# Scan work shared out anew, two second-mixer stages merged, and constant products on TensorE in waits of the norm and choice stages

## The chip, the cores and the metric

The kernel runs on one core of one Trainium2 chip. The metric is the device time of one execution in microseconds, as the median of several runs. A profile of one execution gives, beside it, what every engine did: TensorE (PE, with its weight loads as PEld), VectorE (DVE), ScalarE (ACT), GpSimd (POOL), SyncE (SP), and the transfers.

## The reference

Two transformer blocks for one sequence of 512 tokens of width 1024, all in float32. The first block's mixer is a neighbourhood attention beside a bidirectional state-space scan; its feed-forward part has 16 experts that each choose 64 tokens. The second block's mixer adds a recurrent branch (RWKV-7, 8 heads of 64) and latent attention (8 heads, causal); its feed-forward part has 4 groups of 8 experts, with one group and two experts a token. The parts that matter here, shortened:

```
# scan, per direction, chunk of 128 tokens and group g (R = 8 heads of 64, state 128)
x = xs * dt;  a = dt * A;  a_cs = cumsum(a)
states = B^T @ (exp(a_cs[-1] - a_cs) * x)              # what a chunk adds to the state
h = exp(a_cs[-1]) * h + states                         # decay, then add
y_diag = (C @ B^T) * exp(segment sums of a, masked) @ x
y_off  = exp(a_cs) * (C @ h_before)
# the context (2 chunks) only sets the first state; the main sequence (4 chunks) gives y

# second mixer
y = groupnorm(rwkv(...)) * gn_w + gn_b + bonus * v;  y = y * g
q_d, kv_d, kr = h @ w_in[:, mla columns]               # "down", 384 + 256 + 32 columns
q = rmsnorm(q_d) @ w_q_up;  kv = rmsnorm(kv_d) @ w_kv_up;  rotary part by cos and sin of positions
u = gate_rw * (y @ w_branch_rw) + gate_mla * (attention(q, kv) @ w_branch_mla);  x = x + u @ w_out

# choices
aff = softmax(h @ w_router); each expert takes its 64 largest of 512 tokens       # first block
group = argmax(softmax(h @ w_group)); the two largest of the group's 8 experts    # second block
```

## The kernel before

The program is a row of stages. A stage (`stage(k, name)`, an `nc.Block`) has one instruction list for each engine, its own tiles in SBUF and PSUM and its own semaphores; at its end the semaphores are freed and all engines meet at a barrier. Inside a stage the lists are written by hand, and only semaphores order them; `Steps` chains each instruction of an engine to the one before. Tiles are laid out with 128 tokens (P) to a partition block; LT = 4 blocks make the sequence, KD = 8 blocks the width. A product of f32 operands shows in the profile as two pairs of weight load and matmul.

**Scan** (`ssd_scan`, from L1226). `units` lists 48 units: for both directions, first two context chunks and then four main chunks, each with 4 groups. `mains` are the 32 main units, `chain` = 8 is the number of units between two of one direction and group (4 groups in 2 directions), so the first 8 units only copy their state product and the other 40 decay and add. For each unit GpSimd writes `seg_in` (main units, L1277: a triangular constant times `a`, 128x1024), `xd` (L1283) and `xde` (L1286). TensorE computes, for main units, `seg` (L1300, 4 matmul records) and `cb` (L1302) one unit ahead, then `st` (L1313, the state product), `yo` (L1318) and the 8 heads' `yd` (L1323). ScalarE exponentiates `seg` into `lx` (L1334). VectorE masks `cb` (L1345), multiplies `lx` by it (L1349), copies (L1354) or decays (L1358) and adds (L1359) the state, and makes y from `off` and `yd` (L1362 to L1371); the second direction has one more add, onto the first direction's y. There are two buffers each of `seg_in`, `xd`, `xde`, `lx`, `off` and one `st`.

**Norm rows** (`RowNorm`, used by the stages `route`, `mixer_rows` and `hm_choose`). VectorE and ScalarE normalize 4 row blocks, the last instruction of each is L322; in the first two stages a branch is added first. `row_ready` counts them. TensorE's `turn` then waits for all four, transposes the 8 column blocks (L370, 4 transposes each) and calls a callback for each, in the choosing stages the scores (L2149, L3318).

**Choices.** `route_tokens`: after the scores VectorE and ScalarE make `aff`, TensorE turns it (L2157), VectorE finds 64 of 512 by rounds of 8 (L2196, L2197), TensorE turns the choice back (L2161) and counts (L2167). `route_experts` (`hm_choose`): VectorE's choices, then TensorE's counts (L3328, L3331). `fine_experts` (`hm`): TensorE makes two lists (L3479), GpSimd gathers rows by indirect transfers (L3462), TensorE turns them (`flips`, L3487) and multiplies with a ring of weights (L3501). The weights of both groups of experts are asked for by SP as early as their buffers allow.

**Second mixer** (`second_mixer`, L3174). Around the change the stages follow in this order: `rw_states` (L2693), `rw_finish` (L2757: VectorE's group norm in 24 us, one square root on ScalarE, the bonus on GpSimd; SP loads the norm rows, the first branch weights into `ahead` and the residual), `rw_y_t` (transposes of y, L402), `rw_br` (branch product, 8 products of 8 records by L526, and multiply onto `uT`, L1539), a load of constants, `p_mla` (the down projection, 8 products of 16 records, width 336), `mla_rows` (L2816: ScalarE's squares, sine and roots, VectorE's rotary tables and normalized rows, 3 tables turned), `mla_qn_t` and `mla_kvn_t` (20 transposes, L402), `mla_up` (L2905, which loads its two weights itself), then attention. `ahead` is a pair of weight buffers that a stage fills for the next one.

## Time and profile before

| what | value |
|---|---|
| median of 3 runs | 3734.84 us (3734.08 to 3745.22) |
| the profiled execution, own time | 3730.5 us |
| its span | 3728.7 us |
| TensorE busy | 3155.3 us, 85% |
| TensorE weight loads | 1675.7 us, 45% |
| VectorE busy | 1146.8 us, 31% |
| ScalarE busy | 478.1 us, 13% |
| GpSimd busy | 320.3 us, 9% |
| instructions | 38059 |
| read from and written to HBM | 653.28 MB, 14.69 MB |

The span runs from the first to the last instruction of the profiled execution; the busy shares are means over stages with different limits. The granted clock of TensorE is given in parts of its full rate: 1.00 is 2.4 GHz and 0.50 is 1.2 GHz. Idle time in brackets stands before an instruction, with what ended it.

### The profile page before, as it was taken

To read this page: it belongs to the slowest core of one execution; us is meant where nothing else is said; L and a number is where in the kernel's file an instruction comes from. 1 tells how busy PE (TensorE), PEld (TensorE's weight loads), DVE (VectorE), ACT (ScalarE), POOL (GpSimd) and SP (SyncE) were. 2 spreads that over 40 slices of the span, in tenths; PEclk is the share of its full clock that TensorE was granted. 3 is DMA by queue.
4 is the path that set the end of the run, shared out by engine and by line. 5 is a ranking of instruction groups with operands and counts; after the bars stand their busy time and mean duration, and the time that the engine had idled before them with its cause. 6 is when DMAs were issued, how large, how long until landed. Compare 5 with 4: busy or idle time off the path is not lost. (4 is left out here: it accounts for less than half of the span.)

```text
span 3728.7 us, 38059 instructions
## 1 busy us (share of the span) xinstructions
PE 3155.3 (85%) x15800; PEld 1675.7 (45%) x15800; DVE 1146.8 (31%) x2119; ACT 478.1 (13%) x898; POOL 320.3 (9%) x261
## 2 busy tenths in 40 slices
PE   6997799996989999598999999987967577995974
PEld 4444545562654444444434443434447443534331
DVE  2234602554893200401011101113264613512112
ACT  1002500111112100100000000001123101301111
POOL 0003000003972000000000000000012100000000
PEclk9998998996999999699999999998989788995997
DMA  6621021100001221399999999995100120015996
GB/s 255 248 68 46 1 71 46 46 23 1 23 1 68 90 68 45 159 410 418 423 416 423 415 428 424 423 388 179 34 1 3 52 76 24 23 45 215 398 425 277
DMA packets 130497, 669.34 MB, mean 180 GB/s; under 512 B 15994, under 2 KB 44061, under 8 KB 97305
## 3 DMA queue, kind: packets, MB, share of 16 engines
q1 hardware_dynamic: 115385, 630.24, 42.1%
q10 hardware_dynamic: 11488, 28.31, 2.0%
q0 software_dynamic: 3456, 8.39, 0.6%
q8 instruction: 125, 2.05, 0.2%
q14 instruction: 43, 0.35, 0.0%
HBM read 653.28 MB, written 14.69 MB: 179 GB/s over the span
## 5 line engine op out<-in xcount | busy, mean ns | idle before, releaser
L1907 PE MATMUL ec_wide<-ec_ring,ec_xg 128*64 128x512 f32 x2048 | 457.9, 601 | 24.3 <-issue 18.6
L1907 PEld LDWEIGHTS ec_wide<-ec_ring,ec_xg 128*64 128x64 f32 x2048 | 148.2, 138 | 313.9 <-issue 309.7
L1941 PE MATMUL ec_acc<-ec_ring,ec_hidT 128*64 128x512 f32 x1024 | 232.8, 608 | 38.4 <-DMA ec_ring<-in_w_exp_down 36.3
L2066 DVE TENSOR_SCALAR ec_xg<-ec_piece,ordered 128x128 f32<-128x128 f32 x64 | 21.9, 404 | 583.0 <-PE ec_piece L1955 583.0
L1941 PEld LDWEIGHTS ec_acc<-ec_ring,ec_hidT 128*64 128x64 f32 x1024 | 84.5, 140 | 184.6 <-issue 184.6
L3501 PE MATMUL hm_gu<-hm_ring,hm_xg 128*64 128x512 f32 x480 | 110.8, 615 | 23.7 <-DMA hm_ring<-in_moe_w_gu 22.3
L1955 PE MATMUL ec_piece<-ec_sel,x 128*128 128x128 f32 x512 | 124.4, 405 | 3.3 <-DVE ec_sel L2048 3.3
L1955 PEld LDWEIGHTS ec_piece<-ec_sel,x 128*128 128x128 f32 x512 | 122.9, 336 | 9.1 <-issue 5.7
L2631 POOL TENSOR_TENSOR solve_T<-const_rw,solve_T 128x512 f32<-128x512 f32 x8 | 10.1, 1266 | 1330.2 <-DVE solve_T L2669 1330.2
L1107 PE MATMUL conv_main<-hT,conv_early 128*128 128x512 f32 x192 | 85.3, 599 | 1.6 <-DVE bcT L1183 1.6
L526 PE MATMUL p_rkv_acc<-ahead_rkv,h2mT 128*128 128x384 f32 x256 | 84.5, 494 | 2.3 <-DVEq L534 2.3
L1107 PE MATMUL conv_main<-hT,conv_late 128*128 128x512 f32 x192 | 85.8, 600 | 0.0
L2030 ACT ACTIVATE ec_hidT<-ec_acc 128x512 f32<-128x512 f32 x32 | 17.4, 594 | 519.3 <-PE ec_acc L1930 519.3
L3501 PEld LDWEIGHTS hm_gu<-hm_ring,hm_xg 128*64 128x64 f32 x480 | 39.2, 141 | 94.3 <-issue 92.5
L1277 POOL TENSOR_TENSOR ssd_seg_in<-const_all,a 128x1024 f32<-128x1024 f32 x32 | 77.3, 2416 | 0.6 <-PE ssd_cb L1302 0.6
L2081 DVE TENSOR_TENSOR branch<-branch,ec_piece 128x512 f32<-128x512 f32 x64 | 44.0, 687 | 107.2 <-PE ec_piece L1973 107.2
L1973 PE MATMUL ec_piece<-ec_y,ec_selT 128*128 128x512 f32 x128 | 63.8, 622 | 7.3 <-DVE ec_selT L2075 6.1
L1286 POOL TENSOR_TENSOR ssd_xde<-ssd_xd,dec 128x512 f32<-128x512 f32 x48 | 68.7, 1431 | 3.8
L1300 PE MATMUL ssd_seg<-ssd_seg_in,const_all 128*128 128x512 f32 x128 | 62.4, 610 | 4.7 <-DVE ssd_cbm L1345 4.7
L526 PEld LDWEIGHTS p_rkv_acc<-ahead_rkv,h2mT 128*128 128x128 f32 x256 | 49.4, 193 | 37.0 <-DVEq L534 2.5
L2676 DVE TENSOR_TENSOR solve_T<-solve_T,solve_wide 64x512 f32<-64x512 f32 (+1 forms) x80 | 50.5, 632 | 50.0 <-PE solve_wide L2562 42.0
L1358 DVE TENSOR_TENSOR ssd_state<-ssd_state,dec 128x512 f32<-128x512 f32 x40 | 59.7, 1492 | 18.4 <-PE ssd_st L1313 18.4
(620 smaller groups left out, 5016.5 us busy)
## 6 DMA issues: line engine op xcount, KB each, us to landing
ec_ring<-in_w_exp_gate SPq DMA_DIRECT2D x64, 2048.0 KB, 14.0
ec_ring<-in_w_exp_up SPq DMA_DIRECT2D x64, 2048.0 KB, 22.2
ec_ring<-in_w_exp_down SPq DMA_DIRECT2D x64, 2048.0 KB, 17.7
hm_ring<-in_moe_w_gu SPq DMA_DIRECT2D x30, 2048.0 KB, 18.8
hm_ring<-in_moe_w_down SPq DMA_DIRECT2D x15, 2048.0 KB, 15.9
ahead_qkv<-in_w_in SPq DMA_DIRECT2D x10, 2048.0 KB, 9.6
key<-in_w_ada ACTq DMA_DIRECT2D x4, 2048.0 KB
v<-in_w_ada ACTq DMA_DIRECT2D x4, 2048.0 KB, 10.2
```

What stands on the lines that cost most here:

```text
L526: last = pe.matmul(acc[0:rows, bank, 0:cols], stat(j), mov(j), start=(j == 0), stop=(j == kt - 1))
L1107: last = pe.matmul(main[:, i % 2, :], w[:, j, m * P:(m + 1) * P], hT[:, j, :], start=(j == 0), stop=(j == KD - 1))
L1277: pool.tensor_tensor(seg_in[:, m % 2], cum.unsqueeze(1).to_broadcast([P, HG, P]), spread(a[:, tile(u), hs:hs + HG], P), ALU.mult).then_inc ...
L1286: pool.tensor_tensor(xde[:, n % 2].rearrange("p (h e) -> p h e", h=HG), xd[:, n % 2].rearrange("p (h e) -> p h e", h=HG), spread(e2, 64), ...
L1300: pe.matmul(seg[:, h, :], k.const("after" if d == 0 else "before"), seg_in[:, m % 2, 4 * h:4 * h + 4].rearrange("p h l -> p (h l)"), start ...
L1358: link(dve.tensor_tensor(sv, sv, spread(e3, 64), ALU.mult))
L1907: last = pe.matmul(wide[half(e), b, :], xg[:, u % 2, j, half(e)], w[e][:, a, b * 512:(b + 1) * 512], start=(j == 0), stop=(j == KD - 1))
L1941: last = pe.matmul(acc[half(e), h, :], hidT[:, f, half(e)], w[e][:, r, h * 512:(h + 1) * 512], start=(f == 0), stop=(f == FT - 1))
L1955: last = pe.matmul(piece[:, m % 2, i * P:(i + 1) * P], x[:, t, HALF * h + i::KD], sel[:, t, :], start=(t == 0), stop=(t == LT - 1))
L1973: pe.matmul(piece[:, m % 2, :], selT[:, t * P:(t + 1) * P], y[:, h * 512:(h + 1) * 512], start=True, stop=True).then_inc(piece_done, 1)
L2676: dve.tensor_tensor(x, x, wide[s][half(c), c, first * 256:512], ALU.subtract).then_inc(T_done[s], 1)
L3501: last = pe.matmul(gu[half(e), u % 2, :], xg[:, u % 2, j, half(e)], w[e][:, j, :], start=(j == 0), stop=(j == KD - 1))
```

## The change

Three parts. **Scan:** `seg_in` is written by ScalarE, two units ahead, as eight 128x128 activations with a per-partition scale; the state decay goes from VectorE to GpSimd, between the inputs of the next unit and those after it, with a semaphore of its own; the last 8 units, whose state nobody reads, have no `xde`, no state product and no state update. **Second mixer:** SP issues the down weights, the norm rows, positions, constants and residual during `rw_states`; one stage, `rw_finish_and_down`, has the down projection on TensorE, ScalarE's copies of it and the norm on VectorE; a second, `rw_branch_and_rows`, has y's transposes, the branch products, the tables, the normalized rows and all turns, with the branch weights, the two `mla_up` weights and the gate weights asked for by its SP. Seven stages and a load become two stages; two barriers are new in `latent_attention` and `second_mixer`. **Constant products:** `keep_warm(n)` issues n products of `ones` and `ident`, whose result nobody reads, while TensorE waits: after the first, second and third ready row (20 each in `route` and `mixer_rows`, 6 each in `hm_choose`), 12 before `aff`, 72 before the choice, 48 before the counts of `hm_choose` and 64 before the flips of `hm`.

```diff
+def keep_warm(k, pe, bank, n):
+
+    for _ in range(n):
+        pe.matmul(bank[:, 0:P], k.const("ones"), k.const("ident"), start=True, stop=True)
...
+        for t in range(LT - 1):
+            pe.wait_ge(self.row_ready, t + 1)
+            keep_warm(self.k, pe, self.pt[:, 3, :], 20 if self.branch is not None else 6)
...
-            m = 0
-            for n, u in enumerate(units):
-                main, d, c, g = u
+
+            def inputs(n):
+                main, d, c, g = units[n]
                 x = (xs if main else xsc)[:, c, g * GW:(g + 1) * GW].rearrange("p (h e) -> p h e", h=HG)
                 hs = d * SSD_H + g * HG
-                if main:
-                    if m >= 2:
-                        pool.wait_ge(seg_ready, m - 1)
-                    cum = k.const("upto" if d == 0 else "from")
-                    pool.tensor_tensor(seg_in[:, m % 2], cum.unsqueeze(1).to_broadcast([P, HG, P]),
-                                       spread(a[:, tile(u), hs:hs + HG], P), ALU.mult).then_inc(seg_built, 1)
                 if n >= 2:
-                    pool.wait_ge(state_ready, n - 1)
+                    if n - 2 < kept:
+                        pool.wait_ge(state_ready, n - 1)
                     if n - 2 in mains:
                         pool.wait_ge(diag_ready, mains.index(n - 2) + 1)
-                link(pool.tensor_tensor(xd[:, n % 2].rearrange("p (h e) -> p h e", h=HG), x,
-                                        spread(dt[:, tile(u), hs:hs + HG], 64), ALU.mult))
-                e2 = dec[:, d * N_SEG + tile(u), 32 + g * HG:32 + (g + 1) * HG]
+                ins = pool.tensor_tensor(xd[:, n % 2].rearrange("p (h e) -> p h e", h=HG), x,
+                                         spread(dt[:, tile(units[n]), hs:hs + HG], 64), ALU.mult)
+                if n >= kept:
+                    ins.then_inc(inputs_ready, 1)
+                    return
+                link(ins)
+                e2 = dec[:, d * N_SEG + tile(units[n]), 32 + g * HG:32 + (g + 1) * HG]
                 pool.tensor_tensor(xde[:, n % 2].rearrange("p (h e) -> p h e", h=HG),
                                    xd[:, n % 2].rearrange("p (h e) -> p h e", h=HG), spread(e2, 64),
                                    ALU.mult).then_inc(inputs_ready, 1)
-                m += main
+
+            def decayed(n):
+                main, d, c, g = units[n]
+                if main:
+                    pool.wait_ge(off_ready, mains.index(n) + 1)
+                pool.wait_ge(state_done, n - chain + 1)
+                e3 = dec[:, d * N_SEG + tile(units[n]), 64 + g * HG:64 + (g + 1) * HG]
+                sv = state[:, d, g, :].rearrange("p (h e) -> p h e", h=HG)
+                pool.tensor_tensor(sv, sv, spread(e3, 64), ALU.mult).then_inc(state_decayed, 1)
+
+            inputs(0)
+            for n in range(len(units)):
+                if n + 1 < len(units):
+                    inputs(n + 1)
+                if chain <= n < kept:
+                    decayed(n)
...
+                if n < kept:
+                    if n >= 1:
+                        pe.wait_ge(state_done, n)
+                    pe.matmul(st[:, :], (b_rows if main else bc_rows)[:, c, g * P:(g + 1) * P], xde[:, n % 2, :], start=True,
+                              stop=True).then_inc(state_ready, 1)
+                else:
+                    pe.wait_ge(state_done, n - chain + 1)
...
+            def segment_inputs(m):
+                main, d, c, g = units[mains[m]]
+                if m >= 2:
+                    act.wait_ge(seg_ready, m - 1)
+                cum = k.const("upto" if d == 0 else "from")
+                for h in range(HG):
+                    col = d * SSD_H + g * HG + h
+                    ins = act.activation(seg_in[:, m % 2, h, :], cum, ACT.Copy, scale=a[:, tile(units[mains[m]]), col:col + 1])
+                ins.then_inc(seg_built, 1)
+
+            segment_inputs(0)
+            segment_inputs(1)
             for m in range(len(mains)):
                 act.wait_ge(seg_ready, m + 1)
                 if m >= 2:
                     act.wait_ge(diag_ready, m - 1)
                 act.activation(lx[:, m % 2].rearrange("p (b h) l -> p b (h l)", b=2), seg[:, :, :], ACT.Exp).then_inc(exped, 1)
+                if m + 2 < len(mains):
+                    segment_inputs(m + 2)
...
-                dve.wait_ge(state_ready, n + 1)
+                if n < kept:
+                    dve.wait_ge(state_ready, n + 1)
                 if n < chain:
                     dve.tensor_copy(state[:, d, g, :], st[:, :]).then_inc(state_done, 1)
-                else:
-                    e3 = dec[:, t, 64 + g * HG:64 + (g + 1) * HG]
-                    sv = state[:, d, g, :].rearrange("p (h e) -> p h e", h=HG)
-                    link(dve.tensor_tensor(sv, sv, spread(e3, 64), ALU.mult))
+                elif n < kept:
+                    dve.wait_ge(state_decayed, n - chain + 1)
                     dve.tensor_tensor(state[:, d, g, :], state[:, d, g, :], st[:, :], ALU.add).then_inc(state_done, 1)
...
+            keep_warm(k, pe, norm.pt[:, 0, :], 12)
             pe.wait_ge(aff_ready, 1)
...
+            keep_warm(k, pe, norm.pt[:, 0, :], 72)
             pe.wait_ge(chosen_T, 1)
...
+        @block.tensor
+        def _(pe):
+            for i, (c, t) in enumerate(tiles):
+                if t == 0:
+                    pe.wait_ge(down_loaded[c], 16)
+                if i >= 4:
+                    pe.wait_ge(product_taken, i - 3)
+                for j in range(KD):
+                    last = pe.matmul(acc[:, i % 4, 0:width], hT[:, j, t * P:(t + 1) * P], down_w[:, c, j * width:(j + 1) * width], start=(j == 0), stop=(j == KD - 1))
+                last.then_inc(product_ready, 1)
+
         @block.scalar
         def _(act):
-            act.wait_ge(var_ready, 1)
-            act.activation(var[:, :, :], var[:, :, :], ACT.Sqrt, scale=1.0 / 64, bias=k.const("gn_eps")).then_inc(root_ready, 1)
+            for i, (c, t) in enumerate(tiles):
+                act.wait_ge(product_ready, i + 1)
+                act.activation(down[:, t, c * width:(c + 1) * width], acc[:, i % 4, 0:width], ACT.Copy).then_inc(product_taken, 1)
+                if i == 2:
+                    act.wait_ge(var_ready, 1)
+                    act.activation(var[:, :, :], var[:, :, :], ACT.Sqrt, scale=1.0 / 64, bias=k.const("gn_eps")).then_inc(root_ready, 1)
+            act.wait_ge(product_taken, len(tiles))
...
+            for b in range(2):
+                ahead.load_first(sp, b, k.dram["w_branch_rw_2"][0], NY, 512)
+            for (dst, src), up_loaded in up_moves:
+                sp.dma_start(dst, src).then_inc(up_loaded, 16)
+            for b in range(2):
+                sp.wait_ge(product_ready, 4 * (b + 1))
+                ahead.load_first(sp, b, *w_next)
...
+            merge(0)
...
+            for j in range(NY):
+                turn(j, lambda t: y[:, t, j * P:(j + 1) * P], P).then_inc(y_flipped, 1)
+            pe.wait_ge(y_taken, NY)
+            for m in range(3):
+                product(m)
             pe.wait_ge(table_ready, 2)
             for i in range(3):
-                for t in range(LT):
-                    last = pe.transpose(bank[0:MLA_QK, i, t * P:(t + 1) * P], table[:, i, t, :], k.const("ident"))
-            last.then_inc(flipped, 1)
-
-
-def mla_up(k, qnT, kvnT, cT, sT, krT, qT, kT, v):
+                turn(i, lambda t: table[:, i, t, :], MLA_QK).then_inc(flipped, 1)
+            product(3)
+            for i, (dst, scale, j) in enumerate(columns):
+                source = qn if i < MLA_Q // P else kvn
+                pe.wait_ge(normed, LT if i < MLA_Q // P else 2 * LT)
+                if i:
+                    pe.wait_ge(flip_taken, i)
+                turn(3 + i, lambda t: source[:, t, j * P:(j + 1) * P], P).then_inc(flipped, 1)
+                if i in (1, 3):
+                    product(4 + i // 2)
+            product(6)
+            product(7)
...
+                    def late_loads(sp):
+                        for b in range(2):
+                            source = w_down.rearrange("(k p) n -> p k n", p=P)[:, :, b * (n_down // 2):(b + 1) * (n_down // 2)]
+                            sp.dma_start(down_w[:, b].rearrange("p (k n) -> p k n", k=KD), source).then_inc(down_loaded[b], 16)
+                        for dst, name in zip(norm_rows, ("rw_gn_w_2", "rw_gn_b_2")):
+                            sp.dma_start(dst[:, :], k.dram[name][0:1, :].to_broadcast([P, RW_D])).then_inc(norm_loaded, 16)
+                        sp.dma_start(pos_i[:, :], k.dram["positions_2"].rearrange("a (t p) -> p (a t)", p=P),
+                                     allow_slow_non_contiguous=True).then_inc(positions_loaded, 16)
+                        sp.dma_start(*mla_const).then_inc(mla_const_loaded, 16)
+                        sp.dma_start(k.residual.tile[:, :, :], rows_view(x_in)).then_inc(k.residual.loaded, 16)
+                        sp.wait_ge(mla_const_loaded, 16)
+
+                    rw_states(k, MT, N, D_next, GT, K_[:, :, :].rearrange("p t (c q n) -> p (t c) q n", q=RW_PAIRS, n=64), y, late_loads)
+                    rw_finish_and_down(k, y, z, g, bonus, Q, norm_loaded, norm_rows, hT, (down_w, down_loaded), down)
...
-                rw_finish(k, y, z, g, bonus, branch_loads)
...
-                yT = tile(s, "rw_yT", [P, RW_D // P, L])
-                transpose_rows(k, "rw_y_t", y, LT, RW_D // P, yT)
-                branch(k, "rw_br", k.dram["w_branch_rw_2"][0], RW_D // P, yT, uT, None, False, ahead, (w_down, KD, n_down // 2))
...
+            keep_warm(k, pe, norm.pt[:, 0, :], 48)
             pe.wait_ge(chosen_ready, 1)
...
+            pe.wait_ge(index_ready, 2)
+            keep_warm(k, pe, list_, 64)
             flips(0)
```

## Rows read from the trace of the kernel before

**Rows 1.** The page, section 2: busy tenths of the transfers in 40 slices.
```profile
DMA  6621021100001221399999999995100120015996
```

**Rows 2.** Stretch, us, busy (count) of PE, PEld, DVE, ACT, POOL; clock, DMA share, GB/s.
```profile
939.00:1036.00 97.00, 96.69 (x453) 61.72 (x453) 85.57 (x106) 18.42 (x18) 89.65 (x53) 1.00 0.00 1
...
1515.40:1535.80 20.40, 20.27 (x96) 19.77 (x96) 3.26 (x5) 4.39 (x5) 0.00 (x0) 0.50 0.86 367
...
2549.00:2553.80 4.80, 4.76 (x23) 4.76 (x24) 1.69 (x3) 1.37 (x2) 0.00 (x0) 0.50 0.00 0
2553.80:2555.90 2.10, 1.35 (x11) 1.11 (x10) 1.31 (x2) 1.37 (x2) 0.00 (x0) 0.95 0.00 0
```

**Rows 3.** Timeline, context units of the scan: start, duration (us), operation, idle before.
```profile
902.31 0.69 DVE L1354 COPY ssd_state<-ssd_st 128x512 f32<-128x512 f32 x1 [2.30 <-PE ssd_st L1313]
905.30 1.56 DVE L1358 TENSOR_TENSOR ssd_state<-ssd_state,dec 128x512 f32<-128x512 f32 x1 [2.30 <-PE ssd_st L1313]
...
909.88 1.56 DVE L1358 TENSOR_TENSOR ssd_state<-ssd_state,dec 128x512 f32<-128x512 f32 x1 [2.30 <-PE ssd_st L1313]
...
905.27 1.04 POOL L1283 TENSOR_TENSOR ssd_xd<-xsc,dt 128x512 f32<-128x512 f32 x1 [0.82 <-PE ssd_st L1313]
```

**Rows 4.** Timelines, main units of the scan, by engine.
```profile
944.07 1.02 ACT L1334 ACTIVATE ssd_lx<-ssd_seg 128x1024 f32<-128x1024 f32 x1 [2.63 <-PE ssd_cb L1302]
...
1031.17 1.02 ACT L1334 ACTIVATE ssd_lx<-ssd_seg 128x1024 f32<-128x1024 f32 x1 [4.42 <-PE ssd_cb L1302]
1037.16 1.02 ACT L1334 ACTIVATE ssd_lx<-ssd_seg 128x1024 f32<-128x1024 f32 x1 [4.97 <-PE ssd_cb L1302]
...
1126.71 1.02 ACT L1334 ACTIVATE ssd_lx<-ssd_seg 128x1024 f32<-128x1024 f32 x1 [6.09 <-PE ssd_cb L1302]
...
1071.95 0.68 DVE L1358 TENSOR_TENSOR ssd_state<-ssd_state,dec 128x512 f32<-128x512 f32 x1
...
1077.72 2.38 DVE L1358 TENSOR_TENSOR ssd_state<-ssd_state,dec 128x512 f32<-128x512 f32 x1
...
1076.68 2.88 POOL L1277 TENSOR_TENSOR ssd_seg_in<-const_all,a 128x1024 f32<-128x1024 f32 x1
...
1003.64 1.87 PEld L1323 LDWEIGHTS ssd_yd<-ssd_xd,ssd_lx 128*128 128x128 f32 x16
```

**Rows 5.** Timeline, from the states to latent attention, and the weights' landing.
```profile
2959.05 2.29 DVE L2797 TENSOR_REDUCE rw_fin_mean<-rw_y 128x32 f32<-128x2048 f32 x1 [1.65 <-PEq L3247]
...
2970.48 0.32 ACT L2792 ACTIVATE rw_fin_var<-rw_fin_var,const_all 128x32 f32<-128x32 f32 x1 [10.19 <-DVE rw_fin_var L2802]
...
2984.30 3.49 PE L402 MATMUL rw_y_t_pt<-const_all,rw_y 128*128 128x128 f32 x16 [27.69 <-PEq L209]
...
2989.54 2.81 PE L526 MATMUL rw_br_b_acc<-rw_yT,ahead 128*128 128x512 f32 x6 [1.75 <-DVEq L534]
...
3025.34 3.14 PE L526 MATMUL p_mla_acc<-ahead,h2mT 128*128 128x336 f32 x5 [8.10 <-DVEq L534]
...
3063.31 0.51 DVE L546 COPY mla_down<-p_mla_acc 128x336 f32<-128x336 f32 x1 [4.01 <-PE p_mla_acc L526]
...
3100.02 4.55 PE L2946 MATMUL mla_up_pq<-mla_qnT,mla_up_wq 128*96 128x512 f32 x6 [10.94 <-DMA mla_up_wkv<-in_mla_w_kv_up]
...
ahead<-in_w_in SPq DMA_DIRECT2D x2, 1344.0 KB, 5.8
```

**Rows 6.** Timeline: the first ready row, and waits of TensorE in the choosing stages.
```profile
1505.89 0.75 DVE L322 TENSOR_SCALAR branch<-x,ec_rstd 128x1024 f32<-128x1024 f32 x1
...
1537.40 1.02 PE L2157 MATMUL route_wide<-const_all,ec_aff 128*16 128x128 f32 x4 [1.59 <-DVE ec_aff L2190]
...
1551.84 0.60 PE L2161 MATMUL route_score<-const_all,route_chosenT 16*128 16x16 f32 x4 [13.42 <-DVE route_chosenT L2198]
...
3392.76 1.49 PE L3328 MATMUL hm_choose_count<-hm_choose_chosen,const_all 128*128 128x32 f32 x6 [9.03 <-DVE hm_choose_chosen L3389]
...
3419.97 1.97 PE L3487 MATMUL hm_flip<-const_all,hm_xrow 128*128 128x128 f32 x8 [10.06 <-DMA hm_xrow<-hm_xn_rows,hm_index]
```

155 lines of the change are left out of this document (93 added, 62 removed).

## The prediction

> **What bounds the kernel now.** I read the page first: no engine is busier than TensorE (the table above), but the transfers fill slices 18 to 25 and 37 to 38 whole [rows 1]. Those are the two groups of expert stages, in which the weights' transfer is the bound. A stage in front of them that ends later or earlier moves them whole, because their buffers are full by then and the queue stands; no delay ahead of them is made good behind them. Next I cut the run at the stages that the change touches [rows 2]. In the scan's first half TensorE is busy 96.7 of 97 us; in the route stage's turn and scores it is busy throughout at a granted clock of 0.50 (1.2 GHz). The second mixer's turn starts at 0.50 and reads 0.95 after 2553.8. Then I read the timelines: the scan's context units [rows 3] and main units [rows 4], the way from the second mixer's states to latent attention's first product [rows 5], and the waits of TensorE that the constant products are to fill [rows 6].
>
> **Rates.** A 128x128 f32 product is two records (the steps of one f32 product); so one record each counts below. At the raised clock 16 records take 1.87 us [rows 4], 0.117 each; at 0.50 96 take 20.27 [rows 2], 0.211 on the mean and 0.22 by the gap-free ones among them. So a constant product costs 0.23 us raised and 0.44 low.
>
> **A, the scan.** (1) *Context units.* For the first eight, which only copy, starts lie 2.99 apart; for the eight that decay, 4.58 (905.30 to 909.88), with the decay at 1.56 in the chain of VectorE and TensorE [rows 3]. With the decay on GpSimd the chain is the copy's 2.99 again, since the add costs as the copy, but GpSimd must do three multiplies of one size, for which I take the 1.04 of the one in these rows [rows 3], and 0.2 between them: 3.3. The bound above is the decay at VectorE's 1.56, and the other way the copy's 2.99. So 8 x (4.58 - 3.3) = -10; bounds -6 and -13. (2) *Main units, first half.* 16 periods from 944.07 to 1031.17 are 5.44 each [rows 4], and TensorE has no gap [rows 2]: nothing is gained. GpSimd loses 2.3 us of segment inputs and gains 1.04 of decay; what hides it is TensorE's own 5.44. (3) *Second half.* 13 periods from 1037.16 to 1126.71 are 6.89 each [rows 4]. There VectorE has one more add, and its two-input operations stretch: the decay takes 0.68 at 1071.95, and 2.38 at 1077.72 while GpSimd's 1024-wide multiply runs from 1076.68 for 2.88 [rows 4]. Removed are that multiply and the decay. In the first half VectorE keeps TensorE's pace of 5.44 with all of these operations but one, and the decay goes, so 5.44 would be the bound here too; but the mask, for which TensorE waits, stands behind the additional add, and for that I put 0.5 (the add is no longer than the 0.68 of the decay alone): 5.95. 16 x 0.93 = -15; bounds 0 and -23. The last eight units' missing state products give nothing in this sum: VectorE's order sets them. (4) *ScalarE.* It takes eight 128x128 activations a unit. None of this size and form stands in these rows: the 128x32 one takes 0.32 [rows 5] and the 128x1024 one 1.02 [rows 4]. I take 0.35, near the small one by size: 8 x 0.35 + 1.02 = 3.8, inside the 5.44 of TensorE, and two units ahead. At the other end, 1.02, it is 9.2 (see the rivals). A together: **-25**, bounds -15 and -33 (the ends aren't met together).
>
> The Trainium skill ("SBUF — State Buffer", the two sides) says that VectorE's two-input operations and GpSimd's reads take one port pair as an exclusive lock, for a whole instruction. The 2.38 beside the 0.68 agrees. It speaks against the move as well: decay on GpSimd locks VectorE out for its whole length.
>
> **B, the second mixer.** Before, the way is a chain without overlap: VectorE's finish starts at 2959.05 and hands on at 2984.30; y's transposes; branch products from 2989.54, which end at 3025.34 - 8.10 = 3017.24; a load and 8.10 idle; the down projection from 3025.34 to 3063.31; the rows and tables, two transposing stages, and a wait of 10.94 for weights that only mla_up asks for, to 3100.02 [rows 5]. From 2957.4 (the last product of the states) that is 142.6. After: the finish's stage starts at 2958.4 (one barrier less before it). TensorE's 64 products of 336 columns take 38.0 (3063.31 - 3025.34), to 2996.3, ScalarE's last copy to 2996.9. VectorE's 24.4 lies beside it; its root, at 2970.48 before [rows 5], now waits for ScalarE's third copy at 2958.4 + 3 x 4.74 + 0.5 = 2973 or later, 2.5 to 4.3 late: VectorE ends by 2987.7, hidden by 9 us. Two barriers: 2998.5. Now SP issues the branch weights, which stood loaded before: 1344 KB takes 5.8 to land [rows 5]; I take 5.5 for the 1024 KB, so 3004.0 (below: 3.5, what 16 transposes at 0.22 need anyway; above: 7.5). Eight products took 27.7 (2989.54 to 3017.24); 12 + 20 transposes at 0.112 to 0.23 add 3.6 to 7, waits and the low clock's start 1 to 2: 3037. The tables' chain (ScalarE's squares, table load and sine, VectorE's rows) starts when the stage does. In these rows it stands with two transposing stages and their barriers between 3063.8 and 3100.02 - 10.94 = 3089.1 [rows 5], 25.3 in all, which bounds it; I take 14 of them, to 3012.5. The third product ends at 3004.0 + 3 x 3.46 = 3014.4, so it is hidden, but by little. Last merge and barrier: mla_up starts at 3038.7, its weights asked for long before. So -61.3; two more barriers inside latent attention +1.8, and mla_up's first products at the raised clock -1.6: **-61**, bounds -50 (tables 11 late at 25.3) and -64 (weights at 3.5).
>
> **C, the constant products.** *Cost.* In route and mixer TensorE is free for products when the first row is ready: 1505.89 + 0.75 = 1506.64 [rows 6]; the turn starts at 1515.4 [rows 2]. Sixty products, the first 8 to 15 low, take 15.1 to 16.8, longer than the 8.8 of the rows: the turn is 6.3 to 8 late, I take 7.2, in each of the two stages (the mixer's has the same spacing). The choice's 18 products: 2.4 late (1.6 to 3.3). The 12 behind the scores (2.7 raised) stand against a wait of 1.59 [rows 6]: +1.8 with a slower hand-over (1.1 to 3.7). The 72 take 16.5 against 13.42: +3.5 (2.7 to 6). The 48 take 10.8 against 9.03: +1.8. The 64 behind the lists take 16 to 17.7 against 10.06: +7.0 (6 to 8) [rows 6]; VectorE's gathered rows are late by as much. Together 30.9. *Return.* If the clock is up when the turn starts, the 20.3 us of turn and scores shrink [rows 2]; 12 records a tile at 0.117 and two hand-overs make about 11.6, but a dip is likely: -6 in route and -8 in the choice stage (-2 to -8.7 each). The mixer's turn, 6.1 to 6.8, falls to 4.3: -2.5, as the 0.95 after 2553.8 shows a raised turn to go [rows 2]. The counts behind 72 and 48: -2.2, -2.7. The flips, and the experts' first products behind 64: -3.4; p_rkv's first: -0.9. Together -25.7. Net **+5**, bounds -8 and +20.
>
> The Trainium skill ("TensorE: Matmul & The Clock Gate", LDWEIGHTS) states that loading the stationary operand takes its columns over 1.2 in ns, without the clock in it. By it a turn, half loads, would give back little. Here 16 load records took 1.87 us at clock 1.00 and 96 took 19.77 at 0.50, 0.117 and 0.206 each [rows 2, 4], so the trace disagrees; by the rule the sum would be some 18 higher.
>
> **Sum.** -25 - 61 + 5 = -81. The profiled execution took 3730.5 by its own clock (span 3728.7): 3649.5. The runs' median, 3734.84, lies 4.3 above it: **3652**.
>
> **Rivals.** (1) *The clock gives nothing back* (this is the change not doing what it says): 30.9 is paid and the 25.7 lost, +26: 3678. For it: the score stage stayed at 0.50 with TensorE busy throughout [rows 2]. Against it: the mixer's transposes raised it to 0.95 [rows 2]. 0.12. (2) *The scan yields only its context part*: GpSimd's decay, multiply and multiply (3.1 at least) meet VectorE's two-input operations in the second half and stretch them as the 2.38 does [rows 4]; the period stays 6.7: 16 x 0.75 lost, 3664. 0.12. (3) *The merged stage waits*, for its tables or the branch weights: B is -45, 3668. 0.08. (4) *Better*: A at -33 and C at -4: 3635. 0.05. (5) *Slower*: ScalarE bounds the scan. At 1.02 an activation [rows 4] a unit takes 9.3; 32 units make 298 for the 197 of now, +101 on -56 - 10: 3770. It decides from 0.92 each, where 8 x 0.92 + 1.02 + 0.2 = 8.6 a unit eats the other gains and 11 us. Against it: 0.32 for the small one [rows 5]. 0.03, and 0.01 for a size between.
>
> **How the numbers follow.** The forecast has 0.59; its own range is 3638 to 3668. For 8 in 10 the range takes in rivals 2 to 4 and most of 1: 3626 to 3686 (A, B and C at their low ends are -105, 3630, less 4 if the median lies no higher than the profiled execution; B at -50 and C at +20 with A at -19 are 3686). 0.3% is 11 us, about what a measurement of this kernel can tell from no change. Only rival 5 reaches that: faster 0.96, same 0.01, slower 0.03.
>
> **What would show it.** A: context units at 3.3, main units at 5.44 and 5.95, ScalarE's activations at 0.35; wrong if ScalarE has no idle time or the second half reads 6.7. B: the down projection beside the finish, 38 us; third branch product before the tables; mla_up's first product 81 us after the states' last; wrong if TensorE idles before the tables' turn. C: granted clock near 1.00 in turn and scores and the route's turn late by 7; wrong if the clock there reads 0.50, or if the idle of TensorE before the counts stays. The prediction fails most easily at C's return and at the second half of the scan.

## The result, and the profile after

The changed kernel takes 3647.07 us (median of 4, 3644.0 to 3661.75) where the kernel before takes 3736.16 on the same chip: ratio 0.9765, 95% interval 0.9733 to 0.9796, so faster by 2.0 to 2.7%. The forecast was 3652, range 3626 to 3686. Executions of one kernel differ by up to 19 us; so single parts of the change are read from the stages of the traces, and the medians only for what is larger.

The page after, its first section, and the granted clock by slices:

```profile
span 3642.8 us, 39461 instructions
PE 3197.3 (88%) x16452; PEld 1725.6 (47%) x16452; DVE 1071.7 (29%) x2059; ACT 559.0 (15%) x1166; POOL 274.7 (8%) x253
PEclk9998998997999999999999999998998989998997
```

TensorE has 652 matmul records more and 42 us more busy time in a span 86 us shorter. The constant products are 668 records and 85.1 us of it (16 records of state products are gone, and the other records took 43 us less); busy time is no gain in itself. ScalarE went from 478.1 to 559.0, GpSimd from 320.3 to 274.7, VectorE from 1146.8 to 1071.7.

Where the span's 85.9 us come from, by the same marks in both traces (a fourth row is the end of the norm's last instruction; the other marks are starts; the first experts end with their last `ec_acc` product, the second with the output's last row; the states' last product and `mla_up` are TensorE's):

| stretch | before | after | difference | forecast |
|---|---|---|---|---|
| scan, start to first `lx` (context part) | 63.37 | 53.22 | -10.15 | -10 |
| to the 18th `lx` (first half) | 90.75 | 91.01 | +0.26 | 0 |
| to the 32nd `lx` (second half) | 95.54 | 83.60 | -11.94 | -15 |
| to the last head products | 6.45 | 7.54 | +1.09 | 0 |
| route, fourth row to the first gather | 45.14 | 43.45 | -1.69 | +4.3 |
| first experts | 956.41 | 952.34 | -4.07 | 0 |
| mixer, fourth row to `p_rkv` | 8.46 | 13.92 | +5.46 | +3.8 |
| states' last product to `mla_up` | 143.6 | 82.3 | -61.3 | -61.3 |
| `mla_up` to attention's turned output | 159.76 | 163.25 | +3.49 | +0.2 |
| choice, fourth row to the lists | 42.49 | 33.85 | -8.64 | -6.5 |
| lists to the first expert product | 17.40 | 23.73 | +6.33 | +3.6 |
| second experts | 299.81 | 295.44 | -4.37 | 0 |

The last column has the terms of the prediction put to these marks; what the table leaves out, -0.3, is spread over the stages between.

The context units after, GpSimd's timeline, beside [rows 3]:

```profile
903.51 1.04 POOL L1306 TENSOR_TENSOR ssd_state<-ssd_state,dec 128x512 f32<-128x512 f32 x1
904.51 1.04 POOL L1288 TENSOR_TENSOR ssd_xd<-xsc,dt 128x512 f32<-128x512 f32 x1
905.63 1.04 POOL L1295 TENSOR_TENSOR ssd_xde<-ssd_xd,dec 128x512 f32<-128x512 f32 x1
906.63 1.04 POOL L1306 TENSOR_TENSOR ssd_state<-ssd_state,dec 128x512 f32<-128x512 f32 x1
```

GpSimd has no gap; three multiplies make a unit, 3.12 us instead of 4.58. The second half after, beside [rows 4], TensorE, VectorE, GpSimd and ScalarE:

```profile
1054.18 1.96 PE L1324 MATMUL ssd_seg<-ssd_seg_in,const_all 128*128 128x512 f32 x4 [0.31 <-DVE ssd_cbm L1386]
...
1101.77 1.96 PE L1324 MATMUL ssd_seg<-ssd_seg_in,const_all 128*128 128x512 f32 x4 [1.10 <-DVE ssd_cbm L1386]
...
1052.20 0.69 DVE L1410 TENSOR_TENSOR ssd_off<-ssd_off,ssd_yd 128x512 f32<-128x512 f32 x1
1052.92 0.91 DVE L1411 TENSOR_TENSOR y<-y,ssd_off 128x512 f32<-128x512 f32 x1
1053.75 0.28 DVE L1386 TENSOR_TENSOR ssd_cbm<-ssd_cb,const_all 128x128 f32<-128x128 f32 x1
...
1054.69 2.02 POOL L1306 TENSOR_TENSOR ssd_state<-ssd_state,dec 128x512 f32<-128x512 f32 x1
...
1050.40 1.02 ACT L1373 ACTIVATE ssd_lx<-ssd_seg 128x1024 f32<-128x1024 f32 x1 [2.64 <-PE ssd_cb L1326]
1051.32 2.43 ACT L1364 ACTIVATE ssd_seg_in<-const_all,a 128x128 f32<-128x128 f32 x8
1056.39 1.02 ACT L1373 ACTIVATE ssd_lx<-ssd_seg 128x1024 f32<-128x1024 f32 x1 [2.64 <-PE ssd_cb L1326]
```

A unit is 5.99 here and 5.97 on the mean of the stretch. The last periods, whose units have no state product, are 5.93: TensorE's gap there is 1.10, again up to the mask, so that leaving these products out gave next to nothing here. ScalarE's eight small activations take 2.43 together, 0.30 each, and it is idle for 2.64 a unit. In the units before, TensorE's one gap is 0.31 and ends with the mask, which stands behind two adds of VectorE.

The merged stages, TensorE's timeline, beside [rows 5]:

```profile
2936.97 36.40 PE L2839 MATMUL rw_fin_acc<-rw_T,h2mT 128*128 128x336 f32 x128 [1.84 <-PEq L209]
2975.49 2.86 PE L2988 MATMUL mla_rows_flip<-const_all,rw_y 128*128 128x128 f32 x16 [2.12 <-PEq L3383]
2981.01 13.30 PE L2998 MATMUL mla_rows_acc<-mla_o,ahead 128*128 128x512 f32 x24 [2.66 <-DMA ahead<-in_w_branch_rw]
2994.15 1.47 PE L2988 MATMUL mla_rows_flip<-const_all,mla_v 128*96 128x128 f32 x12
2995.46 3.60 PE L2998 MATMUL mla_rows_acc<-mla_o,ahead 128*128 128x512 f32 x8
...
3017.21 3.62 PE L3058 MATMUL mla_up_pq<-mla_qnT,mla_wq 128*96 128x512 f32 x4 [2.23 <-PEq L209]
```

TensorE is idle for 1.84, 2.12, 2.66 and 2.23 us, at the three boundaries and for the branch weights, 8.9 of the 82.3 us. The tables are turned at 2994.15 without a wait. The turn and the scores of both choosing stages, busy time by stretch beside [rows 2] (first the bursts in front of them):

```profile
1484.80:1499.90 15.10, 15.06 (x121) 15.06 (x122) 7.89 (x12) 3.36 (x9) 0.00 (x0) 0.89 1.01 430
1499.90:1511.10 11.20, 10.66 (x98) 10.33 (x96) 3.25 (x4) 4.01 (x5) 0.00 (x0) 1.00 1.01 430
...
3285.80:3296.90 11.10, 10.69 (x98) 10.38 (x97) 3.00 (x4) 3.65 (x5) 0.00 (x0) 1.00 0.99 392
```

20.3 us have become 11.2 at a granted clock of 1.00. The turn starts 6.3 us after the fourth row in route and 7.7 in the mixer.

### The profile page after: what moved, and what is told of

Same layout as the page of the kernel before. It is cut to its first block and busy times, and to the rows that moved or that the text cites. A ratio compares the mean times of both kernels' runs of the same rounds, so it can differ in the third digit from the quotient of the medians.

```text
span 3642.8 us, 39461 instructions
## 1 busy us (share of the span) xinstructions
PE 3197.3 (88%) x16452; PEld 1725.6 (47%) x16452; DVE 1071.7 (29%) x2059; ACT 559.0 (15%) x1166; POOL 274.7 (8%) x253
## 5 line engine op out<-in xcount | busy, mean ns | idle before, releaser
L1981 PE MATMUL ec_acc<-ec_ring,ec_hidT 128*64 128x512 f32 x1024 | 233.9, 611 | 36.4 <-DMA ec_ring<-in_w_exp_down 34.2
L1364 ACT ACTIVATE ssd_seg_in<-const_all,a 128x128 f32<-128x128 f32 x256 | 77.8, 390 | 1.8 <-PEq L1766 1.8
L1350 PE MATMUL ssd_yd<-ssd_xd,ssd_lx 128*128 128x64 f32 x512 | 62.1, 275 | 2.1 <-DVE ssd_lx L1390 2.1
L535 PE MATMUL na_br_g_acc<-hT,ahead_na 128*128 128x512 f32 x128 | 57.2, 610 | 7.1 <-ACTq L543 7.1
## 6 DMA issues: line engine op xcount, KB each, us to landing
ec_ring<-in_w_exp_down SPq DMA_DIRECT2D x64, 2048.0 KB, 17.5
hm_ring<-in_moe_w_down SPq DMA_DIRECT2D x15, 2048.0 KB, 15.3
v<-in_w_ada ACTq DMA_DIRECT2D x4, 2048.0 KB, 10.2
```

Source lines behind the costliest of these rows:

```text
L535: last = pe.matmul(acc[0:rows, bank, 0:cols], stat(j), mov(j), start=(j == 0), stop=(j == kt - 1))
L1350: last = pe.matmul(yd[:, m % 2, h * 64:(h + 1) * 64], lx[:, m % 2, h, :], xd[:, n % 2, h * 64:(h + 1) * 64], start=True, stop=True)
L1364: ins = act.activation(seg_in[:, m % 2, h, :], cum, ACT.Copy, scale=a[:, tile(units[mains[m]]), col:col + 1])
L1981: last = pe.matmul(acc[half(e), h, :], hidT[:, f, half(e)], w[e][:, r, h * 512:(h + 1) * 512], start=(f == 0), stop=(f == FT - 1))
```

## The experiments

All start from the changed kernel. Marks as in the table above.

**No constant products** (`a1_no_constants`):

```diff
-    for _ in range(n):
+    for _ in range(0):
```

> All constant products out, the rest of the changed kernel kept. Theory 1 (what the stages of the trace after show is all they do: route -1.7, mixer +5.5, choice stage up to the first expert product -2.3, so +1.5 net; the 4.1 and 4.4 us by which the two expert stretches are shorter have another cause): 3646, and both expert stretches stay short. Theory 2 (the shorter expert stretches come from them as well, -8.5 more): 3654, and the first expert stretch is back at 956 us, the second at its old length. The forecast's +5 would make it 3642.

Measured: 3653.0, ratio 0.9767 (0.9745 to 0.9790), the same as with them. Route 45.21 (43.45 with them), mixer 9.08 (13.92), choice 42.68 (33.85), lists to first expert product 17.37 (23.73): in these stages the constant products cost 0.6 us altogether, so they give and take in about equal parts. The experts' stretches are 959.7 and 296.6. The second stayed short, against theory 2. The first is nearly what theory 2 has (956), and so is the median (3654), but this decides nothing: with the products in, other traces of the changed kernels have 951.7 to 965.7 there. Turn and scores are back at 20.3 and 0.50:

```profile
1494.70:1515.00 20.30, 20.25 (x96) 19.73 (x96) 3.24 (x4) 4.39 (x5) 0.00 (x0) 0.50 0.89 376
```

**No 64 before the flips** (`a2_no_64`):

```diff
-            keep_warm(k, pe, list_, 64)
```

> Only the 64 products before the first flips out. Theory 1 (forecast: a delay in front of the experts is carried to the end): flips 7.3 us earlier, flips and first products 3.3 slower at the low clock, end 4 earlier: 3643. Theory 2 (the ring's transfers start with the stage and are the bound from there, so that a late flip is made good): the first expert product is 4 us earlier and the end is where it was, 3647 within 1.

Measured: ratio 0.9767 (0.9747 to 0.9787). Lists to the first expert product 17.31 instead of 23.73, lists to the end of the second experts' stretch 311.8 instead of 319.2: the 6.4 us stay won, so theory 1, with more than the 4 us of its sum. With the 64 products the flips (1.06 for 8 records, 1.94 here) and the first experts' products are faster, but the end is no earlier for it. TensorE waits for the gather again as in [rows 6]:

```profile
3334.27 1.94 PE L3615 MATMUL hm_flip<-const_all,hm_xrow 128*128 128x128 f32 x8 [10.00 <-DMA hm_xrow<-hm_xn_rows,hm_index]
```

The median, 3647.9, doesn't show it; with 4 executions 6 us can't be told from chance.

**No burst in the mixer** (`a3_no_mixer_burst`) and **bursts of 8** (`a4_burst_of_8`):

```diff
-            keep_warm(self.k, pe, self.pt[:, 3, :], 20 if self.branch is not None else 6)
# a3 (only route has a shift)
+            keep_warm(self.k, pe, self.pt[:, 3, :], 20 if self.shift is not None else 0 if self.branch is not None else 6)
# a4
+            keep_warm(self.k, pe, self.pt[:, 3, :], 8 if self.branch is not None else 6)
```

> The 60 products of the second mixer's norm stage out, those of the route stage kept. Theory 1 (they are 7.7 us late and give back 2.4 in the turn and under 1 behind it): the way from the fourth row to the first p_rkv product is 8.5 us instead of 13.9 and the end 4.5 to 5.5 earlier: 3642. Theory 2 (what follows is bound by a load, not by TensorE): no change of the end, 3647.

> Bursts of 8 instead of 20 in the route and mixer stages: 8 products at the low clock are 3.6 us, the spacing of the rows, so the third burst ends 2 us behind the fourth row. Theory 1 (that is enough for the clock): turn and scores stay at 11.3 us in route and 3.7 in the mixer, both turns start 4 to 5.5 us earlier: 3638. Theory 2 (the clock is not up at the turn): turn and scores take 15 to 20 us again, the mixer's turn 5 to 6: 3647 to 3650.

Measured: 3645.9 and 3648.8, ratios 0.9766 (0.9738 to 0.9793) and 0.9758 (0.9736 to 0.9780), neither to be told from the changed kernel. By the traces the mixer's way is 8.41 with none (9.08 in `a1_no_constants`), 6.65 with 8 (in three traces) and 12.4 to 14.2 with 20 (in eight). So 8 are enough there, and the other 12 only delay. In route, in the one trace with 8, the stage took 45.45; the clock fell among the scores, 0.63 on the mean:

```profile
1495.40:1512.40 17.00, 16.53 (x98) 16.30 (x98) 3.24 (x4) 4.39 (x5) 0.00 (x0) 0.63 1.00 424
```

Theory 1 holds for the mixer. For route this trace is as theory 2 has it; but with 20 the clock falls among the scores too in some traces (see `c1_joined`), so one trace doesn't show that 8 are too few.

**Decay back on VectorE** (`s1_decay_on_vector`):

```diff
-                if chain <= n < kept:
-                    decayed(n)
...
-                    dve.wait_ge(state_decayed, n - chain + 1)
+                    link(dve.tensor_tensor(sv, sv, spread(e3, 64), ALU.mult))
```

> The state decay back on VectorE, the segment inputs still on ScalarE. Theory 1 (the forecast's shares: the decay's move made the context part, the segment inputs' move the second half): context part 10 us longer again, first half at 5.44 a unit, second half at 6.0 to 6.7 because the decay costs VectorE 0.7 alone and meets a shorter GpSimd load; end 10 to 21 later: 3657 to 3668. Theory 2 (it is the pair that counts: without the 1024-wide multiply GpSimd hardly stands in VectorE's way and the second half needs nothing else): second half stays at 5.97, 3657.

Measured: ratio 0.9796 (0.9780 to 0.9813), 3657.9. Context part 63.33, as before the change; first half 90.75; second half 83.51, as after it. That is theory 2. VectorE's decay, with GpSimd's 1024-wide multiply gone:

```profile
1049.68 1.75 DVE L1388 TENSOR_TENSOR ssd_lx<-ssd_lx,ssd_cbm 128x1024 f32<-128x1024 f32 x1
1051.35 0.68 DVE L1398 TENSOR_TENSOR ssd_state<-ssd_state,dec 128x512 f32<-128x512 f32 x1
...
1048.98 1.37 POOL L1295 TENSOR_TENSOR ssd_xde<-ssd_xd,dec 128x512 f32<-128x512 f32 x1
```

It takes 0.68 in each of the second half's seven decays, where it alternated between 0.68 and 2.38 in [rows 4]. In the context part and the first half it still takes 1.56 and 1.48 on the mean, as before, beside GpSimd's other multiplies. So the segment inputs' move made the second half without the decay's. The reverse case is the next run.

**Segment inputs back on GpSimd** (`s2_segments_on_gpsimd`), decay there too:

```diff
+                    if n + 1 in mains:
+                        seg_inputs(mains.index(n + 1))      # the 128x1024 multiply of before
...
-                    segment_inputs(m + 2)
```

> The segment inputs back on GpSimd as one 1024-wide multiply, the decay still on GpSimd. Theory 1 (GpSimd becomes the bound: 2.3 + 1.0 + 1.4 + 1.4 a unit and blocking): context part as after, first half 6.2 to 6.6 a unit instead of 5.46, second half 6.9 to 7.5: 3676 to 3690. Theory 2 (TensorE and VectorE still bound the first half, since the inputs are made ahead): first half 5.5, second half as before the change, 6.9: 3659.

Measured: ratio 0.9817 (0.9794 to 0.9840), 3671.5. Context 53.53, first half 96.93, second half 89.98. The periods are 5.84 in the first half, 6.29 in the second as long as units have a state product, and 6.56 in the last ones. Neither theory has these numbers: the second half is shorter than theory 2's 6.9 and theory 1's range. Up to the last units GpSimd is busy without a gap (139.2 of 141.4 us), which is theory 1's cause at less than its price:

```profile
1054.21 1.89 POOL L1305 TENSOR_TENSOR ssd_seg_in<-const_all,a 128x1024 f32<-128x1024 f32 x1
1056.06 1.04 POOL L1288 TENSOR_TENSOR ssd_xd<-xs,dt 128x512 f32<-128x512 f32 x1
1057.18 1.37 POOL L1295 TENSOR_TENSOR ssd_xde<-ssd_xd,dec 128x512 f32<-128x512 f32 x1
1058.51 2.02 POOL L1315 TENSOR_TENSOR ssd_state<-ssd_state,dec 128x512 f32<-128x512 f32 x1
```

In the last units GpSimd is idle half the time (22.1 of 45.0 us busy); there VectorE's multiply, beside the 1024-wide one of GpSimd, and the mask hold the unit:

```profile
1095.31 2.34 POOL L1305 TENSOR_TENSOR ssd_seg_in<-const_all,a 128x1024 f32<-128x1024 f32 x1
...
1096.13 2.60 DVE L1397 TENSOR_TENSOR ssd_lx<-ssd_lx,ssd_cbm 128x1024 f32<-128x1024 f32 x1
```

So the decay's move without the segment inputs' gives the context part (-9.8) and, with the last units' missing state work, 5.6 us of the second half, but costs 6.2 in the first: it needs the segment inputs' move, and not the other way round.

**The mask's wait later** (`s3_mask_wait_later`):

```diff
                     pe.wait_ge(exped, m)
-                    pe.wait_ge(masked, m)
...
+                if m >= 1:
+                    pe.wait_ge(masked, m)
                 pe.matmul(cb[:, 0:P], bT...
```

> TensorE's wait for the mask moved from in front of the two segment products to in front of the product of C and B, the only one that needs it. Theory 1 (what holds the second half at 5.97 is the chain last head product, two VectorE adds, mask, segment products): the period falls to between 5.5 and 5.75, the second half is 4 to 7 us shorter: 3641 to 3644. Theory 2 (VectorE's multiply of the masked tile, 1.75 to 2.0 behind the mask, comes last anyway): 5.9 to 5.97, no gain.

Measured: 3645.8, ratio 0.9748 (0.9731 to 0.9766); the median doesn't show it, and the trace lost 4.5 us again in its route stage (47.93). Second half 76.47 instead of 83.60, the last unit 0.85 longer: -6.3. The mean period is 5.46, but no unit has it: the units with a state product take 5.77 and the last ones, without, 5.18. In the former TensorE has no gap (38.6 of 39.0 us busy) and is the bound again; in the latter it waits 0.33 for VectorE's multiply. So the chain of theory 1 did hold the second half, and 5.3 of the 7.1 us came in the last seven periods, where leaving out the state product, which had given nothing, now counts.

```profile
1083.78 2.00 PE L1351 MATMUL ssd_yd<-ssd_xd,ssd_lx 128*128 128x64 f32 x16 [0.33 <-DVE ssd_lx L1391]
```

**Tables first** (`b1_tables_first`):

```diff
-            for m in range(3):
-                product(m)
             pe.wait_ge(table_ready, 2)
             for i in range(3):
                 turn(i, ...)
-            product(3)
+            for m in range(4):
+                product(m)
```

> In the merged stage the three tables are turned before the first branch product and not behind the third. Theory 1 (the tables' chain of ScalarE and VectorE is ready 7.8 us after the weights, and only the three products hide it): the first branch product starts at about 2990.3 instead of 2981.0, mla_up 7.8 us later: 3655. Theory 2 (the chain isn't on the path, TensorE has room later in the stage): mla_up at most 2 later, 3648.

Measured: ratio 0.9791 (0.9771 to 0.9811), 3660.9. States to `mla_up` 91.27 instead of 82.30, +9.0. Theory 1. The median is 14 above that of the changed kernel; what is beyond the 9 lies in stages with the same code (the first experts took 965.7 in this trace). The two waits of TensorE, and its start on `mla_up`:

```profile
2995.24 2.92 PE L2988 MATMUL mla_rows_flip<-const_all,rw_y 128*128 128x128 f32 x16 [2.12 <-PEq L3382]
3008.73 2.77 PE L2988 MATMUL mla_rows_flip<-const_all,mla_v 128*96 128x128 f32 x12 [10.57 <-DVE mla_v L2961]
...
3044.24 1.93 PE L3057 MATMUL mla_up_pq<-mla_qnT,mla_wq 128*96 128x512 f32 x4 [2.23 <-PEq L209]
```

The 10.57 us now stand in the open, and after them the turns run at the low clock (2.77 for what took 1.47).

**One barrier less** (`b2_one_barrier`):

```diff
-        nc.clear_and_free_semaphores([up_loaded])
-        nc.all_engine_barrier(sem_only=True)
...
-                nc.clear_and_free_semaphores([norm_loaded, ...
+                nc.clear_and_free_semaphores([up_loaded, norm_loaded, ...
```

> The barrier between mla_up and attention out, its semaphore freed with the others behind attention. Theory 1 (the added barrier makes TensorE's idle time there longer, the clock falls, and attention's first scores and gate products take twice their time): from mla_up's first product to the transposes of attention's output 160.3 to 161 us instead of 163.25, back near the 159.8 of before. Theory 2 (a barrier costs its own time alone): 162.3 to 162.9.

Measured: 3644.5, ratio 0.9749 (0.9724 to 0.9773); the stretch is 160.31 instead of 163.25. Theory 1. The start of attention, first after the change, then here:

```profile
3071.87 1.59 PE L3125 MATMUL mla_score<-mla_kT,mla_qT 96*128 96x128 f32 x4 [2.15 <-PEq L3239]
...
3075.57 3.46 PE L1635 MATMUL mla_gate_acc<-h2mT,ahead 128*128 128x512 f32 x4
```

```profile
3079.26 0.89 PE L3125 MATMUL mla_score<-mla_kT,mla_qT 96*128 96x128 f32 x4 [1.78 <-PEq L209]
...
3081.95 1.88 PE L1635 MATMUL mla_gate_acc<-h2mT,ahead 128*128 128x512 f32 x4
```

With an idle time of 2.15 instead of 1.78 us everything behind it takes nearly twice its time for about 7 us: a barrier of 0.4 us cost 2.9. This isn't chance: all ten traces with the barrier have the 2.15 and a clock of 0.50 behind it, and the three without it, and the kernel before, have 1.78 to 1.80 and no fall.

**Down projection after the finish** (`b3_down_after_finish`):

```diff
+            pe.wait_ge(finished, 1)          # VectorE, behind its last operation
             for i, (c, t) in enumerate(tiles):
...
+            act.wait_ge(var_ready, 1)        # the root, ahead of the copies and no longer behind the third
+            act.activation(var[:, :, :], var[:, :, :], ACT.Sqrt, ...
```

> In the first merged stage TensorE waits with the down projection until VectorE has finished the norm (the root goes ahead of ScalarE's copies). Theory 1 (the overlap with VectorE's 24.4 us is that much of the gain): states' last product to mla_up's first 82.3 + 24.4 = 107, end 3671. Theory 2 (most of the gain is from boundaries and waits, the overlap brings less since two engines in one stage slow each other): under 100.

Measured: ratio 0.9826 (0.9806 to 0.9845), 3671.5. States to `mla_up` 109.41, +27.1: theory 1, a little more than VectorE's 24.4. Of the -61.3 that is 27. The rest stands in [rows 5] as `mla_up`'s wait (10.9), the idle 8.1, the rows and turns that now lie between the products, and boundaries; no run takes these apart.

**Joined** (`c1_joined`: mask later, no 64, bursts of 20 in route and 8 in the mixer, one barrier less; `c2_joined_14`: 14 in route):

> The changed kernel with the mask's wait later (-6.3 in the stages of its own trace), no 64 products before the flips (-6.4), bursts of 8 in the mixer's norm (-6.6) and one barrier less (-2.4 by theory 1 of that run, -0.6 by theory 2). If the stages add, about 21 us below the changed kernel: 3626, ratio 0.970. Rival (the gains are lost in the expert stretches, whose transfers vary by more): ratio 0.975.

> The same with bursts of 14 instead of 20 in the route stage: 42 products end 3.8 us earlier. Theory 1 (14 keep the clock up through turn and scores as 20 do): from the fourth row to the first gather product 39.6 instead of 43.45. Theory 2 (the clock falls among the scores, as with 8): 42 to 45.5.

Measured: 3633.4 and 3634.1, ratios 0.9725 (0.9708 to 0.9743) and 0.9734 (0.9712 to 0.9755), the lowest of all; the first lies between the full sum (0.970) and its rival (0.975). By their own stages the scan, the mixer (6.65), the barrier (160.30) and the flips (17.5) gave what they had given alone. Of the 21 us 14 came by the medians and 9 by the profiled spans, since in this trace route took 48.01 instead of 43.45 and the first experts 959.8 instead of 952.3. With 14 route took 48.70: the clock fell among the scores, as in theory 2, but the stage is 3 us beyond the range of that theory. The route stage of `c1_joined`:

```profile
1496.90:1509.00 12.10, 11.56 (x99) 11.23 (x98) 3.24 (x4) 4.39 (x5) 0.00 (x0) 0.93 0.83 351
1509.00:1514.00 5.00, 5.00 (x24) 5.00 (x25) 1.07 (x5) 0.26 (x1) 3.51 (x1) 0.50 0.00 0
```

The clock fell inside the scores. It is not the other edits: among the ten traces with 20 in route, six have bursts of 15.2 to 15.3 us together and then a stage of 43.45 to 43.50, and four have 15.4 to 16.6 and a stage of 47.05 to 48.01; the four include runs that change the scan or the second mixer alone. Busy time by stretch around the rise and the fall, first the changed kernel, then `c1_joined`:

```profile
1484.90:1488.10 3.20, 3.20 (x15) 3.20 (x16) 3.10 (x4) 1.01 (x3) 0.00 (x0) 0.50 1.03 440
1488.20:1535.80 47.60, 44.60 (x398) 43.88 (x397) 22.86 (x49) 7.56 (x13) 3.51 (x1) 1.00 0.50 210
```

```profile
1480.50:1486.60 6.10, 6.08 (x28) 6.08 (x29) 5.89 (x8) 1.90 (x6) 0.00 (x0) 0.50 1.01 432
1486.80:1507.10 20.30, 19.83 (x181) 19.59 (x179) 5.07 (x8) 4.40 (x7) 0.00 (x0) 1.00 0.98 416
1507.30:1513.90 6.60, 6.60 (x31) 6.60 (x32) 1.07 (x5) 1.50 (x2) 3.51 (x1) 0.50 0.02 7
```

In the six the clock rose 3.3 to 3.4 us after the first constant product and stayed up through turn, scores and choice. In the four it rose after 3.7 (`b1_tables_first`) or 6.1 to 6.2 us and fell 9.0 or 10.2 us into turn and scores. Why one execution goes the one way and the next the other isn't shown.

## Why the prediction was right, and where it was off

**What held.** The merged mixer is right in its sum (-61.3) and in its mechanisms: VectorE done 8 us ahead of TensorE, its root 4.2 late behind the third copy, the first branch product 5.2 us after the issue of its weights, tables hidden (`b1_tables_first`: +9.0 when they aren't, 7.8 expected), the overlap worth the finish (`b3_down_after_finish`). That the sum is right to a tenth is luck: the down projection took 36.4 for the 38.0 of the forecast, and from the first branch product to `mla_up` it was 36.2 for 34.7. The context units (3.3 expected, 3.12), the second half's period (5.95, 5.97), ScalarE's small activations (0.35, 0.30) and the turn's lateness (7.2; 6.3 and 7.7) are close. Rivals 2, 3 and 5 are refuted: the second half did not stay at 6.7, the merged stage did not wait for its tables and waited for the branch weights no longer than was priced, and ScalarE idles for 2.6 us a unit. That a delay in front of the second experts is carried whole is shown by `a2_no_64`; for the first experts, whose stretch differs by 14 us between traces, no run shows it.

**What was mis-sized.** (1) Scan: -25 was taken, -20.75 came. The difference of periods was right (0.93 taken, 0.92 measured), but I multiplied it by 16 where only the 13 periods from 1037.16 on were long before [rows 4], which gives the -11.9, and the last unit became 1.1 longer. (2) "Two more barriers inside latent attention +1.8, and mla_up's first products at the raised clock -1.6": the second did not come (the first 6 records took 4.48 us, 4.55 before), the first was 3.5, since behind one of the barriers the clock fell. (3) The return in turn and scores was taken at 6 and 8 of at most 8.7 because "a dip is likely"; it was 9.1 and 9.3 in this trace, and what stands behind the scores in route cost 2 us less than was taken. Against that, the mixer's burst of 20 cost 1.7 more, and the 64 products 2.7 more: of the 3.4 that they were to give back, 0.9 came in the flips, and the experts' faster products brought the end no nearer. So C came out at +1.5 by the table (+0.6 beside `a1_no_constants`) and not +5. Over the ten traces with 20 in route that stage takes 45.2 on the mean (six at 43.5, four near 47.7), which is what it takes without any (45.2). So the dip exists, in 4 of 10 executions, and a forecast that allowed for it was not wrong to; no length of burst is seen to pay in route on the mean.

Against the forecast these three are +4, +3 and -4. What makes the measured time shorter than the forecast all the same are the experts' stretches, 4.1 and 4.4 us shorter than before, for which nothing was forecast. That is luck: without it the median would read about 3655, still inside the range. The first of the two stretches reads between 951.7 and 965.7 in the traces of changed kernels, with the same code; so the 956.4 of before is inside that spread and nothing is to be credited. The second reads 293.4 to 296.6 in all of the changed kernels' traces and 299.8 in the one trace of before. `a1_no_constants` shows that most of it is not the constant products (296.6); what it is stays open, and one trace of before can't tell it from chance. The 3652 itself doesn't follow from the sum either: -81 on the median of 3734.84 is 3653.8, and nothing in the working takes the other 1.8 off. One reading of [rows 1] is wrong and changes nothing: the transfers fill slices 18 to 27 and 38 to 39, not 18 to 25 and 37 to 38.

**The clock.** The first rival (clock gives nothing back, 0.12) is refuted by the 11.2 us at 1.00, and by `a1_no_constants`: what the products cost came back but for 0.6. The weight loads shrank with the clock: 96 records took 19.77 us at 0.50 [rows 2] and 10.33 at 1.00, 0.206 and 0.108 each. The Trainium skill's rule for them ("TensorE: Matmul & The Clock Gate", LDWEIGHTS), which has no clock in it, gives for 128 columns an estimate of 107 ns; that agrees at 1.00 and not at 0.50, so the measurement decides. With the 1024-wide multiply off GpSimd, VectorE's decay took 0.68 throughout the second half (`s1_decay_on_vector`), and 1.48 to 1.56 where GpSimd's other multiplies stand beside it. The Trainium skill's rule on the shared port ("SBUF — State Buffer", the two sides) agrees with that.

## What to carry to other kernels

Cut a trace at marks that both kernels have before believing a total: here one part of the change (the constant products) was worth nothing beside two that were worth 21 and 58, and two of its places (the mixer's bursts of 20 and the 64) cost more than they gave. Products that only keep a clock up must fit in the wait that they fill: three bursts of 8 in the mixer's 8.8 us gave 1.8 to 2.4 us, of 20 cost 3 to 6; 64 in a wait of 10 cost 6.4. Fitting isn't enough, though: in route 8 ended 0.4 us behind the fourth row and gave nothing in the one trace. When two engines exchange work, ask of each move alone which stretch it serves; and look at which single instruction a wait really guards, since moving one wait by two lines gave 6.3 us, most of it by making good on work that had been left out before without any gain.

## What the runs showed of the hardware

The rise of the clock is not tied to the program: with the same instructions in route it came 3.3 to 3.4 us after the first constant product in six executions, which kept it through turn and scores, and after 3.7 to 6.2 us in four, in which it fell to 0.50 again 9.0 to 10.2 us into them. In front of attention an idle time of 2.15 us was followed by work at half speed in ten traces of ten, and one of 1.78 to 1.80 in none of four. The length alone doesn't decide: behind the same 2.23 us in front of `mla_up` its first 4 records took 3.62 in the changed kernel and 1.93 in `b1_tables_first`. Eight 128x128 activations with a per-partition scale take 0.30 each when they follow one another, close to the 0.32 of one of 128x32 [rows 5]. GpSimd's 128x1024 multiply took between 1.89 and 2.88 us both before and in `s2_segments_on_gpsimd` (2.31 and 1.89 on the mean of the first half), and its 128x512 decay 1.04 in the context units and up to 2.02 in the main ones, where VectorE has more work: one operation of one shape has no one price.
